# Running sums and their exponentials in place of running products, and a split-format gate projection, in a hybrid encoder block

## The reference

```python
xn = rms_norm(h, norm_pre_mix)
cols = xn @ w_in       # q k v | r k v, low-rank parts | two merge gates
# RWKV-7, forward and backward, 32 heads of 64:
w_log = -softplus(-(w0 + tanh(wd) @ w_up)) - 0.5
decay = exp(-exp(w_log))
a = sigmoid(a0 + ad @ a_up)
k_mod = k * (1.0 + (a - 1.0) * k_a)
S = S * w_t + (S @ a_t) b_t' + v_t k_t' ;  y_t = S @ r_t      # per token
g = sigmoid(gd) @ g_up
o_rwkv = (groupnorm(y_f + y_b) * gain + bias + bonus) * g
mix = (sigmoid(g_attn) * o_attn + sigmoid(g_rwkv) * o_rwkv) @ w_out
h = h + rms_norm(mix, norm_post_mix)
h = h + rms_norm(relu(rms_norm(h) @ w_ffn_up)**2 @ w_ffn_down)
```

## Time and profile before

| | |
|---|---|
| three runs | 1939.5, 1942.8, 1942.93 us; median 1942.8 |
| the profiled execution | 1940.74 us, its span 1938.9 us |
| TensorE busy | 1898.4 us, 98% of the span |
| VectorE busy | 1395.9 us, 72% |
| ScalarE busy | 949.1 us, 49% |
| GpSimd busy | 379.4 us, 20% |
| 700 to 750 us (one pair of the loop) | PE 49.59, DVE 43.55, ACT 25.74, POOL 21.11 us |
| mean granted clock | 0.996 |

### The profile page before, as it was taken

The page is one execution under the profiler, slowest core; times in us unless marked ns, Lnnn a source line. Parts: engine busy times, 40 slices in busy tenths (PEclk is TensorE's granted clock), DMA queues, the critical chain, the costliest instruction groups (busy, mean ns, idle before and its releaser), DMA issues.

```text
span 1938.9 us, 33906 instructions
## 1 busy us (share of the span) xinstructions
PE 1898.4 (98%) x11491; PEld 1659.1 (86%) x11491; DVE 1395.9 (72%) x2502; ACT 949.1 (49%) x1716; POOL 379.4 (20%) x452
## 2 busy tenths in 40 slices
PE   7999999999999999999999999999999999999997
PEld 6888889888888888888888788888888888888886
DVE  5777557888888888888888855856565655656565
ACT  5666544555555555555555445544343444444343
POOL 2000001344444444444444531000000000000001
PEclk9999999999999999999999999999999999999999
DMA  8555766433333333333333237566666665666653
GB/s 239 144 151 150 186 181 170 132 93 86 83 90 93 93 93 93 87 85 84 89 93 95 93 110 239 153 195 188 191 187 194 195 190 186 187 195 194 191 185 122
DMA packets 415371, 281.25 MB, mean 145 GB/s; under 512 B 14075, under 2 KB 372701, under 8 KB 414557
## 3 DMA queue, kind: packets, MB, share of 16 engines
q1 hardware_dynamic: 414560, 277.43, 49.4%
q10 hardware_dynamic: 764, 3.21, 0.4%
HBM read 278.52 MB, written 2.10 MB: 145 GB/s over the span
## 4 chain that ended last, share of the span: by engine, by line
PE 82%; DVE 10%; issue 6%; ACT 0%; POOL 0%; DMA 0%; SPq 0%; DVEq 0%; POOLq 0%; ACTq 0%
PE bank L1730 19%; PE bank L1734 10%; PE bank L1901 9%; PE bank L1749 6%; PE bank L1748 6%; PE bank L1750 6%; PE bank L1903 4%; DVE wlo L919 3%; PE bank L2029 2%; PE bank L2047 2%; PE bank L2052 2%; PE bank L1880 1%; PE bank L1882 1%; PE bank L1881 1%; PE bank L1986 1%
## 5 line engine op out<-in xcount | busy, mean ns | idle before, releaser
L1730 PE MATMUL bank<-xT,whi 128*128 128x512 f32 x1664 | 418.8, 397 | 0.3 <-DVE xT L969 0.3
L1730 PEld LDWEIGHTS bank<-xT,whi 128*128 128x128 f32 x1664 | 303.6, 189 | 56.7 <-DVE xT L969 0.7
L1901 PE MATMUL bank<-xT,whi 128*128 128x512 f32 x1024 | 315.8, 416 | 0.1
L1526 DVE TENSOR_TENSOR wlo<-raw,whi 128x1024 fp32r<-128x1024 f32 x126 | 154.4, 1226 | 162.5 <-ACT whi L878 158.2
L1734 PEld LDWEIGHTS bank<-xT,wlo 128*128 128x128 f32 x1664 | 223.0, 191 | 14.6
L878 ACT ACTIVATE whi<-raw 128x1024 fp32r<-128x1024 f32 x126 | 133.2, 1058 | 205.6 <-PE bank L1750 205.6
L1734 PE MATMUL bank<-xT,wlo 128*128 128x256 f32 x1664 | 227.0, 282 | 0.0
L919 DVE TENSOR_TENSOR wlo<-raw,whi 128x1024 fp32r<-128x1024 f32 (+1 forms) x119 | 181.7, 1539 | 44.4 <-ACT whi L459 40.7
L451 ACT ACTIVATE whi<-raw 128x1024 fp32r<-128x1024 f32 x192 | 201.0, 1047 | 0.0
L1748 PE MATMUL bank<-whi,ft 128*128 128x512 f32 x512 | 199.3, 389 | 0.0
L1749 PE MATMUL bank<-wlo,ft 128*128 128x512 f32 x512 | 199.3, 389 | 0.0
(11 more groups left out here) (252 smaller groups left out, 3493.6 us busy)
## 6 DMA issues: line engine op xcount, KB each, us to landing
raw<-in_w_in SPq DMA_DIRECT2D x106, 1024.0 KB, 6.0
raw<-in_w_ffn_up SPq DMA_DIRECT2D x64, 1024.0 KB, 6.4
raw<-in_w_ffn_down SPq DMA_DIRECT2D x64, 1024.0 KB, 5.0
raw<-in_w_out SPq DMA_DIRECT2D x16, 1024.0 KB, 5.2
raw<-in_w_in SPq DMA_DIRECT2D x4, 768.0 KB, 4.6
xtok<-in_x SPq DMA_DIRECT2D x2, 1024.0 KB, 6.0
upg<-in_g_up SPq DMA_DIRECT2D x16, 128.0 KB, 3.5
hres<-in_x ACTq DMA_DIRECT2D x1, 2048.0 KB, 10.5
```

The costliest lines, as they stand in the source:

```text
L1526: V.tensor_tensor(wlo[:, u % 2, 0:1024], raw[:, (u + 2) % 4, 0:1024], whi[:, u % 2, 0:1024].bitcast(f32), ALU.subtract)
L1730: M(bank[:, :], hi[:, P * k:P * k + P], xT[:, k, :, :], start=k == 0, stop=False)
L1901: M(bank[:, :], hi[:, P * k:P * k + P], xT[:, k, :, :], start=k == 0, stop=False)
```

## The change

- The scans now run in place over `dec` (the tanh of the decay's argument) and add it up, one more per token through `ones`; ScalarE makes the exponentials of the sums into `Pd` (`products`) and of the negated sums into `dec` (`inverses`). `decays_exp`, `inverse` with its reciprocals, and the tile `zero` go.
- kA and kB go: ScalarE makes the affine form of the rate (`key_parts`, into `km`), VectorE multiplies it by k.
- On VectorE `products` stands before the two state chunks, `hats(0)`, `hats(1)` and a half cut stand in the second chunk.
- The gate's up projection: `gah`, `gal` are made once by GpSimd, `ugh` by ScalarE in level 4 and `ugl` by VectorE in level 5 of every pair; TensorE multiplies them in six split-format products. The gate's activations share AS's memory until then.
- `merged_lo` goes from GpSimd to VectorE, in six pieces of two tiles, except for the last three tiles.
- SyncE loads the up weights ahead of the fourth weight load of a pair.
- `scaled_row` for the rows (0,1), (0,2), (0,3) comes later, and TensorE's transposes wait for 2, 4, 6 and 8 rows in place of 5, 6, 7 and 8.

```diff
-        gact = sb("gact", [P, 2, T], stack=mixers)
+        gal = sb("gal", [P, 2, T], f32r, stack=mixers)
+        gah = sb("gah", [P, 2, T], f32r, stack=mixers)
...
+        ugh = sb("ugh", [P, 2, P], f32r, stack=rw)
+        ugl = sb("ugl", [P, 2, P], f32r, stack=rw)
...
+            def pair_units(i, j0=0, j1=4):
+                for j, c0 in tuple(enumerate((RK0, R0, RV0, GR0)))[j0:j1]:
...
-                pair_units(i + 2)
+                pair_units(i + 2, 0, 3)
                 pair_ups(i + 1)
+                pair_units(i + 2, 3, 4)
...
-            def decays_exp(n):
-                act.wait_ge(s["tws"].sem, s["tws"].at(n))
+            def products(n):
+                act.wait_ge(s["plc"].sem, s["plc"].before(n))
+                act.wait_ge(s["ar"].sem, s["ar"].before(n))
                 for d in range(2):
-                    A.activation(dec[d][:], tw[d][:], ACT.Exp, scale=-0.5 * DECAY_E, bias=-0.5 * DECAY_E).then_inc(s["decs"].sem, 1)
+                    act.wait_ge(s["scan"].sem, s["scan"].at(n, d + 1))
+                    A.activation(Pd[d][:, :, 1 - d:P + 1 - d], dec[d][:].rearrange("p (a b) -> p a b", a=2), ACT.Exp,
+                                 scale=-0.5 * DECAY_E, bias=P0LOG).then_inc(s["decs"].sem, 1)
+
+            def inverses(n):
+                for d in range(2):
+                    act.wait_ge(s["decs"].sem, s["decs"].at(n, d + 1))
+                    A.activation(dec[d][:], dec[d][:], ACT.Exp, scale=0.5 * DECAY_E, bias=-P0LOG).then_inc(s["inv"].sem, 1)
...
-                A.activation(kA[:], sh[:, 1, :], ACT.Copy, scale=der[:, bass.ds(64 + n, 1)])
-                A.activation(kB[:], sh[:, 1, :], ACT.Copy, scale=der[:, bass.ds(80 + n, 1)]).then_inc(s["kAB"].sem, 1)
+                act.wait_ge(s["tas"].sem, s["tas"].at(n))
+                for d in range(2):
+                    A.activation(km[d][:], ta[d][:], ACT.Identity, scale=der[:, bass.ds(64 + n, 1)], bias=der[:, bass.ds(80 + n, 1)])\
+                        .then_inc(s["km1"].sem, 1)
...
+                        if n is not None and (l, d) == (4, 0):
+                            w("lg")
+                            act.wait_ge(s["up_ld"].sem, s["up_ld"].n(16 * 5 * n + 80))
+                            A.activation(ugh[:], upg[:], ACT.Copy)
...
-                            decays_exp(n)
                         cut_pair(3, d1, 0)
                         if n is not None:
+                            products(n)
                             rates(n)
                         cut_pair(3, d1, 1)
                         if n is not None:
                             key_parts(n)
+                            inverses(n)
...
-                    w("decs", d + 1)
+                    w("tws")
                     for tb in range(2):
-                        src = dec[d][:, P * tb:P * tb + P]
-                        if d == 0:
-                            x = V.tensor_tensor_scan(Pd[0][:, tb, 1:P + 1], src, zero[:], P0SCALE, ALU.mult, ALU.add)
-                        else:
-                            x = V.tensor_tensor_scan(Pd[1][:, tb, 0:P][:, ::-1], src[:, ::-1], zero[:], P0SCALE, ALU.mult, ALU.add)
+                        t = dec[d][:, P * tb:P * tb + P]
+                        if d == 1:
+                            t = t[:, ::-1]
+                        x = V.tensor_tensor_scan(t, t, ones[:], 0.0, ALU.add, ALU.add)
...
-                    w("tas")
-                    w("kAB")
-                    for d in range(2):
-                        inc(V.tensor_tensor(km[d][:], kA[:], ta[d][:], ALU.mult), "km1")
                     w("nkk")
                     for d in range(2):
                         w("km1", d + 1)
-                        inc(V.tensor_tensor(km[d][:], km[d][:], kB[:], ALU.add), "km2")
+                        inc(V.tensor_tensor(km[d][:], km[d][:], k, ALU.mult), "km2")
 
                         inc(V.scalar_tensor_tensor(ta[d][:], ta[d][:], 1.0, kk[:], ALU.add, ALU.mult), "tt")
-
-                def inverse(self, d):
-
-                    incl = Pd[d][:, :, 1:P + 1] if d == 0 else Pd[d][:, :, 0:P]
-                    self.w("scan", d + 1)
-                    inc(V.reciprocal(blocks(dec[d][:]), incl), "inv")
...
+            def merged_lo(his, k0):
+
+                dve.wait_ge(s["mg_hi"].sem, s["mg_hi"].n(his))
+                x = V.tensor_tensor(xT[:, k0:k0 + 2, 1, :], mrg[:, k0:k0 + 2, :], xT[:, k0:k0 + 2, 0, :].bitcast(f32), ALU.subtract)
+                if k0 % 4 == 2:
+                    x.then_inc(s["mg_lo"].sem, 1)
...
+                        if turning and d == 0 and l >= 5:
+                            merged_lo(l - 4, 2 * (l - 5))
+                        if nx and l == 5 and d == 0:
+                            w("wev", nn)
+                            V.tensor_tensor(ugl[:], upg[:], ugh[:].bitcast(f32), ALU.subtract)
...
+                    nx.products(0)
+                    nx.products(1)
 
                 for c in range(2):
+                    if nx and c == 1:
+                        nx.hats(0)
                     w("ue", c + 1)
                     w("resm", c + 1)
                     inc(V.scalar_tensor_tensor(rhs[:].rearrange("p a b -> p (a b)"), U[:, c, :, :].rearrange("p a b -> p (a b)"), -2.0,
                                                PB[4][:, 0:T], ALU.mult, ALU.add), "rese")
                     if nx and c == 0:
                         nx.keys()
-                        nx.products(0)
-                        nx.products(1)
+                        if turning:
+                            merged_lo(3, 4)
                     elif nx:
-                        nx.inverse(1)
-                        nx.hats(0)
+                        nx.hats(1)
+                        cut_pair(0, d2, 0)
...
-                            nx.inverse(0)
                         dense(0, d2)
+                        if turning:
+                            merged_lo(3, 6)
...
-                nx.hats(1)
-                cut_pair(0, d2, 0)
                 cut_pair(0, d2, 1)
                 dense(1, d2)
+                if turning:
+                    merged_lo(4, 8)
+                    merged_lo(4, 10)
...
-            scaled_row(0, 1)
             rstd_row(1, 7)
-            scaled_row(0, 2)
-            scaled_row(0, 3)
...
+                    scaled_row(0, q + 1)
...
-                    w("scan", d + 1)
+                    w("decs", d + 1)
...
-                                         zero[:].unsqueeze(1).to_broadcast([P, 2, P]), ALU.add)
+                                         ones[:].unsqueeze(1).to_broadcast([P, 2, P]), ALU.mult)
                 x.then_inc(s["asc"].sem, 1)
-                if isinstance(i, int) and i == PAIRS - 2:
-                    merged_lo(0, 0, 4)
-                    merged_lo(1, 4, 8)
...
-                    merged_lo(3, 12, 15)
-                if isinstance(i, int) and i == PAIRS - 2:
-                    merged_lo(2, 8, 12)
+                    merged_lo(12, 15)
...
+            pool.wait_ge(s["up_ld"].sem, s["up_ld"].n(80))
+            pool.wait_ge(s["lo_act"].sem, s["lo_act"].n(4))
+            pool.wait_ge(s["lo_fin"].sem, s["lo_fin"].n(1))
+            Gp.tensor_copy(gah[:], gact).then_inc(s["drv"].sem, 1)
+            Gp.tensor_copy(ugh[:], upg[:]).then_inc(s["drv"].sem, 1)
+            pool.wait_ge(s["drv"].sem, s["drv"].n(9))
+            Gp.tensor_tensor(gal[:], gact, gah[:].bitcast(f32), ALU.subtract).then_inc(s["drv"].sem, 1)
+            Gp.tensor_tensor(ugl[:], upg[:], ugh[:].bitcast(f32), ALU.subtract).then_inc(s["drv"].sem, 1)
...
-                        x = M(PB[2][:, 0:T], upg[:, q, :], gact[:, q, :], start=q == 0, stop=q == 1)
+                        M(PB[2][:, 0:T], ugh[:, q, :], gah[:, q, :], start=q == 0, stop=False)
+                        M(PB[2][:, 0:T], ugh[:, q, :], gal[:, q, :], start=False, stop=False)
+                        x = M(PB[2][:, 0:T], ugl[:, q, :], gah[:, q, :], start=False, stop=q == 1)
...
-            pe.wait_ge(s["lo_fin"].sem, s["lo_fin"].n(1))
+            pe.wait_ge(s["drv"].sem, s["drv"].n(11))
...
-                pe.wait_ge(s["m_h"].sem, s["m_h"].n(5 + k2 // 2))
+                pe.wait_ge(s["m_h"].sem, s["m_h"].n(2 + 2 * (k2 // 2)))
```

More of the change, by code:

```diff
@@ L17 @@
 from contextlib import ExitStack
+import math
 import numpy as np
@@ L38 @@
 P0SCALE = 2.0 ** 56
+P0LOG = 56 * math.log(2.0)
 LV = 7
@@ L157, in block_kernel @@
         lact = sb("lact", [P, 4, T], stack=mixers)
-        gact = sb("gact", [P, 2, T], stack=mixers)
+        gal = sb("gal", [P, 2, T], f32r, stack=mixers)
+        gah = sb("gah", [P, 2, T], f32r, stack=mixers)
         muL = sb("muL", [P, 6], stack=mixers)
         raw4 = sb("raw4", [P, 4, T + 2], stack=mixers)
-        zero = sb("zero", [P, P], stack=mixers)
+        ones = sb("ones", [P, P], stack=mixers)
         der = sb("der", [P, 112], stack=mixers)
@@ L241, in block_kernel @@
         yc = sb("yc", [P, T], stack=rw)
-        ysq = sb("ysq", [P, T], stack=rw)
```

(19 more changed lines are left out.)

24 lines of the change are left out of this document (8 added, 16 removed).

## The result

The changed kernel takes **1929.7 us** in the median of four runs (1927.6 to 1930.0); the kernel before took 1942.7 in four runs beside them (1939.5 to 1942.9). The ratio is 0.9935, with a 95% interval of 0.9917 to 0.9952: faster by 13 us between the medians, and by 11.0 between the two profiled executions (1940.74 and 1929.75; spans 1938.9 and 1927.9). The forecast was 1933.5; its sum for the profiled execution, minus 7.6, became minus 11.0. The 2 us between the two differences are a spread among the executions of the kernel before: those on record at 1939.1 to 1941.2 us have a mean granted clock of 0.996 or 0.997, those at 1942.0 and more 0.995 or 0.996.

A forecast was written before the change was run, and what follows sets the result against it. TensorE, busy 98% of the span, was taken as the bound, through its work, waits and clock. From 1940.74, terms of -2.1 (loop pairs), -3.9, -1.4 and -0.2 gave 1933.1, stated as 1933.5 us; range 1919 to 1940.

The forecast's parts named there:

- Gate products: TensorE's gate projection: two true float products (0.97 us) become six split-format ones (0.80), minus 0.17 per pair.
- The waits before the last two heads groups: End of a loop pair: TensorE's waits of 0.22 and 0.36 us for VectorE's masked copies go, minus 0.58 per pair.
- U: VectorE's sum that TensorE awaits for 0.31 us: lands where it is now; minus 0.1 per pair, ends -0.5 and 0.
- ugl in level 5: New VectorE subtraction ahead of the addition TensorE's level 6 awaits: plus 0.70 us per pair, other end 0.17.
- Pair 14: Turning pair: differences over xT move to VectorE, TensorE's waits and half clock go; -3.9 us, ends -6.5 and -1.
- rival B: The clock: a wait in pair 14's level 5 or before the feed-forward keeps it at half; 1937 us, chance 0.16.
- Before the feed-forward: TensorE's transposes start some 1.7 us earlier, 0.3 is paid for three later rows; -1.4 us, ends -3 and 0.
- A: VectorE slips through: ugl finds the port free and U is early, -1.08 us per pair; 1920 us, chance 0.24.
- C: SBUF port: GpSimd blocks VectorE, whose second subtraction ends after 748.0; slower, 1951 us, chance 0.06.
- D: Nothing measurable: work off VectorE is not on the path, waits are merely renamed; 1940 us, chance 0.04.

The follow-up runs named there:

- cheap inverses: The kernel before the change with each VectorE reciprocal replaced by one cheap scaling of the same tile, leaving wrong factors in dec: 1926.62 us, ratio 0.992.

## Why the prediction was right, and where it was off

The direction and the range held: 1929.7 lies between 1919 and 1940, and three of the four terms of a loop pair came as said. The sum was 3.4 us short: 4.7 in the loop pairs, less 0.7 before the feed-forward, 0.4 at the start of the run, and 0.2 in pair 14, where larger misses cancelled. By its own terms:

- **Gate products, -0.17 per pair: right.** 0.16, by the two runs with and without them. The estimate from the four passes of the Trainium skill (FP8 and Floating Point Precision, TensorE Precision Notes), -0.24, was the worse one. Only the reading of 0.97 was wrong, since the step to the next group is longer than those inside: 1.04 became 0.88.
- **The waits before the last two heads groups, -0.58: right.** Measured -0.61: 0.15, 0.35 and 0.10 inside the last group. The first was read as 0.22 for the reason just given, and the third not counted. The cheap inverses alone remove the same 0.15, 0.35 and 0.10.
- **U, -0.1: this is the step that failed.** "Alternating so [...] from 742.5 I reach the subtraction at 747.1, `hats(1)` and the half cut until 750.2, and U at 750.6: where it is now." On the time scale of the earlier trace rows (2.56 us later than the changed kernel's) the subtraction came at 746.94, nearly as said, the half cut's step was through at 749.76 and U landed at 750.17. From the subtraction to U's start it took 2.82 us, not 3.1: the four operations step in 2.16 when nothing is in the way, and GpSimd, with one product running and one left, added 0.66 (0.13 and 0.53 at the two operations of `hats`), where the forecast's times leave 0.94 for it. U starts 0.2 before the `values` group now, and the whole wait of 0.31 went, with 0.10 behind it: -0.41. I had written that outcome down as the end of the term (-0.5) and chosen the other side.
- **ugl in level 5, +0.70: right, and shown.** 0.68 by the runs that move it, ugl at 0.95 us as forecast (0.9), and at 0.41 once GpSimd stands still. The Trainium skill (SBUF — State Buffer, Who interferes with whom) describes the lock; this case's runs agree, with the subtraction's 0.95 and the cut's 3.41.

The period was to fall by 0.15 and fell by 0.48 (-0.16 - 0.61 - 0.41 + 0.68 = -0.50). U is nearly all of the miss; over 14 pairs it is 4.7 us. 0.4 of it is hidden by the start of the run, which is that much longer ahead of all that the change touches.

- **Pair 14, -3.9: measured -3.7, by luck.** The step to its mark gave -3.65; 0.87 of this belong to pair 13's end, counted above, so -2.8, and its own end gave -0.91 in the step to pair 15. Four terms of it were off. The sum took +1.3 for level 5 and left out the loop's own 0.70, though the text speaks of a wait of 2 us; TensorE came 1.8 later there. The clock fell behind that wait and cost 1.6, which the forecast named as the near end of this term and as part of rival B, and left out of the sum. Against that, U gained its full wait, 1.6 where I took 0.7. And the relief at the heads groups, which I had given away to the two pieces there, came after all, 0.45 of the -0.91 with 0.15 more in the levels behind it; there the new order on VectorE does count, by 0.57. The waits of 0.55 and 2.07 and the half clock behind them went, as said, for 4.6 together (4.3 forecast).
- **Before the feed-forward, -1.4: half of it.** TensorE starts 3.42 us after the first idle product, in place of 5.25 (-1.8, 1.7 forecast), and the clock holds. But it then waits four times for rows of hs, 2.4 us in all: VectorE does scaled rows and low parts from 1204.03 to 1214.9 with one gap of 0.42, and sets the end. I had 0.3 us for the three rows that come later; they cost 1.1 of the 1.8. Net -0.7 by the two traces, -1.0 by the run with the old order.

**The rivals.** A (it slips through, 1920) was nearly right on U (-0.41, -0.5 said) and wrong on the lock; the kernel that it describes is the one with ugl moved, 1918. B had the clock right for pair 14 (1.6 us lost) and wrong before the feed-forward. C did not come: the second subtraction came where I had put it. D is out, by 13 us.

## What to carry to other kernels

An operation's price is set by its place more than by its length: one 0.34 us subtraction cost 0.68 us per pair ahead of the additions, 0.2 in level 6 and nothing where VectorE idles for 2 us. Before adding work to an engine that is not the bound, look for such an idle stretch in its timeline, and for what the engine that it collides with does at that time. And estimate the gain of a lighter engine by the waits on it: 2.6 us less of VectorE per pair (a reciprocal of 1.74 against 0.45, twice) gave the waits, 0.8 us, and 0.2 for products that step slower right behind them, 1.0 us, whether the reciprocals were replaced well or badly, and in the loop pairs the reordering on top gave nothing. Last, check a sum by its terms even when it comes out: pair 14 did, on four wrong ones.

## What the runs showed of the hardware

- VectorE's operations on two SBUF tiles and GpSimd's stretch each other. Beside GpSimd's two pieces of 128x1024 (5.69 us), VectorE's cut of 128x1024 took 3.41 in place of 1.21 and the sum over 128x768 2.80 in place of 0.94; additions that read a PSUM bank stayed at 0.41. One GpSimd piece of 2.85 us held one VectorE instruction back by 2.2. On GpSimd's side the two AS copies took 1.88 in the kernel before, 2.05 beside ugl and 2.40 beside the cut.
- The granted clock fell to its lower level (1.2 GHz) in pair 14 of the changed kernel, behind the wait of 1.73 us in level 5, and stayed there for 3.4 us, though TensorE had work all along then. It did not fall after the waits of 0.7 us in the loop, of 0.88 in pair 14 with ugl in level 6, or of 0.6 and 1.2 before the feed-forward. It fell around waits of 1.83 (pieces on GpSimd), 2.07 (pair 14 before, and with cheap inverses) and 2.41 (before the feed-forward, old order). But the length of the wait does not settle it: with cheap inverses the same wait of 2.41 kept the full clock. Nor is the price fixed: at half speed for 3.4 us in the kernel before and in the changed one, for 6.8 us in pair 14 with the pieces on GpSimd and with cheap inverses.
- An exponential on ScalarE over 128x256 costs about 0.40, a reciprocal on VectorE 1.74. Each pair made two exponentials and two reciprocals of this size; now it makes four exponentials, on an engine that had room (ScalarE's busy time rose from 949.1 to 966.7 us).
